# Sliding-window attention and the start of the gated delta rule: ScalarE takes the output bank, GpSimd's row products are released one by one, and the delta rule's first three steps are issued among the last attention units

## The reference, cut to what matters

```python
mod = c_act @ w_ada + b_ada                  # six vectors of 1024; the last four are made here
# attention, per block n of 128 tokens and head h
s = (q @ k_band.T) * 64**-0.5                # 128 x 256 (128 x 128 for n = 0)
mx = max(s.max(-1), sink); p = exp(s - mx)
out = (p @ v_band) / (p.sum(-1) + exp(sink - mx))
# delta rule, per chunk: products of rows with per-row scalars
kb = k * beta; vb = v * beta; kbG = kb * exp(G); qg = q * exp(G); kdec = k * exp(Glast - G)
m = strict_lower(kb @ k.T * decay); T = inverse(I + m)
v_new = T @ vb - (T @ kbG) @ S; o = qg @ S + (q @ k.T * decay) @ v_new; S = S * exp(Glast) + kdec.T @ v_new
```

## Time and profile before

| | |
|---|---|
| median of 3 runs | 2441.24 us (2441.24 to 2442.61) |
| the profiled execution's own time | 2443.43 us |
| its span | 2441.6 us |
| TensorE busy | 2299.5 us, 94% |
| VectorE, ScalarE, GpSimd busy | 877.3, 681.6 and 671.2 us |
| mean granted TensorE clock | 0.963 |

### The profile page before, as it was taken

The page is one execution under the profiler, slowest core; times in us unless marked ns, Lnnn a source line. Parts: engine busy times, 40 slices in busy tenths (PEclk is TensorE's granted clock), DMA queues, the critical chain, the costliest instruction groups (busy, mean ns, idle before and its releaser), DMA issues.

```text
span 2441.6 us, 31297 instructions
## 1 busy us (share of the span) xinstructions
PE 2299.5 (94%) x12483; PEld 1910.5 (78%) x12484; DVE 877.3 (36%) x1367; ACT 681.6 (28%) x1028; POOL 671.2 (27%) x281
## 2 busy tenths in 40 slices
PE   6997889987999999989999999999999998999998
PEld 5885568876789999968887877888866876888787
DVE  5287644445411111243322033332735524332302
ACT  3253324333100000132222132333325324222212
POOL 0323023422000000024343334333513432444432
PEclk7998889997999999999999999999999998999999
DMA  9214500003168988602322232223313222232222
GB/s 302 69 53 138 173 1 1 1 3 104 61 212 290 303 289 290 216 18 87 103 86 87 104 104 88 86 70 121 105 60 112 90 100 87 86 102 87 87 88 94
DMA packets 220360, 278.01 MB, mean 114 GB/s; under 512 B 9703, under 2 KB 199107, under 8 KB 220260
## 3 DMA queue, kind: packets, MB, share of 16 engines
q1 hardware_dynamic: 211744, 267.49, 33.4%
q10 hardware_dynamic: 7140, 4.87, 0.7%
q0 software_dynamic: 1376, 4.26, 0.5%
HBM read 272.36 MB, written 4.24 MB: 113 GB/s over the span
## 4 chain that ended last, share of the span: by engine, by line
PE 85%; DVE 6%; ACT 2%; issue 1%; SPq 1%; DMA 1%; DVEq 1%; ACTq 1%; POOL 0%; POOLq 0%
PE bank L2517 52%; PE bank L2153 10%; PE bank L2161 5%; PE bank L1601 2%; PE bank L451 1%; PE bank L1909 1%; PE bank L1594 1%; PE bank L3301 1%; PE bank L3320 1%; SPq L353 1%; DMA ring<-in_ffn_w_down 1%; PE bank L2944 1%; PE bank L1552 1%; DMA ring<-in_w_in 0%; PE bank L2924 0%
## 5 line engine op out<-in xcount | busy, mean ns | idle before, releaser
L2517 PE MATMUL bank<-hT_high_split,ring_split 128*128 128x512 f32 x2496 | 799.7, 400 | 3.6 <-DVEq L2631 3.0
L2517 PEld LDWEIGHTS bank<-hT_high_split,ring_split 128*128 128x128 f32 x2496 | 472.2, 189 | 117.5 <-DVEq L2631 3.8
L2517 PE MATMUL bank<-hT_split,ring_split 128*128 128x512 f32 x1248 | 493.3, 395 | 0.0
L2501 POOL TENSOR_TENSOR ring_split<-ring,ring_split 128x2048 fp32r<-128x2048 f32 x60 | 277.3, 4623 | 429.9 <-ACT ring_split L2486 429.9
L2486 ACT ACTIVATE ring_split<-ring 128x2048 fp32r<-128x2048 f32 x108 | 206.9, 1916 | 650.4 <-DMA ring<-in_ffn_w_down 196.4
L2517 PE MATMUL bank<-ring_split,hid_high_split 128*128 128x512 f32 x848 | 272.2, 401 | 10.2 <-DVE hid_low_split L2641 6.9
L2517 PEld LDWEIGHTS bank<-hT_split,ring_split 128*128 128x128 f32 x1248 | 236.2, 189 | 57.3 <-issue 0.2
L2857 POOL TENSOR_TENSOR ring_split<-ring,ring_split 128x2048 fp32r<-128x2048 f32 x40 | 189.7, 4743 | 329.5 <-ACT ring_split L2486 329.5
L2153 PE MATMUL bank<-arena,ring 128*128 x2048 | 236.1, 277 | 5.2 <-issue 5.2
L2153 PEld LDWEIGHTS bank<-arena,ring 128*128 128x128 f32 x2048 | 233.4, 194 | 5.4 <-issue 5.4
L2517 PE MATMUL bank<-ring_split,hid_low_split 128*128 128x512 f32 x576 | 216.4, 400 | 0.8 <-issue 0.8
(11 more groups left out here) (490 smaller groups left out, 2857.9 us busy)
## 6 DMA issues: line engine op xcount, KB each, us to landing
ring<-in_w_in SPq DMA_DIRECT2D x45, 1024.0 KB, 5.2
ring<-in_w_gate SPq DMA_DIRECT2D x32, 1024.0 KB, 5.7
ring<-in_w_up SPq DMA_DIRECT2D x32, 1024.0 KB, 8.2
ring<-in_w_down SPq DMA_DIRECT2D x32, 1024.0 KB, 7.6
ring<-in_ffn_w_gate SPq DMA_DIRECT2D x22, 1024.0 KB, 5.4
ring<-in_ffn_w_up SPq DMA_DIRECT2D x22, 1024.0 KB, 5.3
ring<-in_ffn_w_down SPq DMA_DIRECT2D x22, 1024.0 KB, 4.8
ring<-in_w_ada SPq DMA_DIRECT2D x16, 1024.0 KB, 6.7
```

Of the source, the lines that this page charges most:

```text
L2501: pool.tensor_tensor(low(n), raw(n), high(n).bitcast(F32), ALU.subtract)\
L2517: mm = pe.matmul(dst, left[l], right[r], start=start and n == 0, stop=stop and n == 2)
```

## The change

- **Bank 6 is taken by ScalarE.** A new `take(n)` in `act_swa` copies bank 6 unscaled into `mixed` (once per token block, in the iteration behind the block's last unit) and signals `w_o_taken`. `outputs` on VectorE waits for that signal only, scales inside `mixed` (both operands in SBUF), and moves from j = 1 to j = 3 of the next token block, so two units later.
- **`Pw` has three buffers**, so VectorE's unit u waits for unit u-3's transposes. `ada_sum` moves to make room; some delta rule buffers move by 16 columns.
- **The row products.** The eight of kb and qg now come first, as soon as their inputs are ready. The twelve of vb, kbG and kdec are released one by one: product i waits for VectorE's half of the modulation sum of unit i (`ada_half` behind even units is new). Only `state` is cleared here.
- **The clearing of `vnew`** moves to GpSimd's step 4 of the delta rule, in front of the first L1658 and behind its waits.
- **No meeting.** TensorE issues step 0 of the delta rule behind unit 14's iteration (after waits for `g_scaled`, `g_parts` and `w_s_taken`), step 1 behind iteration 15 and in front of the last values, and the rest behind. ScalarE issues steps 0 and 1 in its iterations 14 and 15, in front of `take(3)`. VectorE issues steps 0 to 2 behind its loop and in front of the last `outputs` and of the end of the modulation vector (`dve_ada2`). GpSimd goes straight on. TensorE's step 11 waits for `w_o_taken` and `mod_ready`.

```diff
-        def meet(e):
-            e.drain().then_inc(S("meet"), 1)
-            nxt(e, "meet", 4)
...
-            if u % 2 == 1:
-                mm.then_inc(S("ada_acc"), 1)
+            mm.then_inc(S("ada_acc" if u % 2 else "ada_half"), 1)
...
-        Pw = region(23616, 1024, "p (b i k) -> p b i k", b=2, i=2)
+        Pw = [region(at, 512, "p (i k) -> p i k", i=2) for at in (23616, 24128, 27216)]
...
+                if u == len(UNITS) - 2:
+                    nxt(pe, "g_scaled")
+                    nxt(pe, "g_parts")
+                    pe.wait_ge(S("w_s_taken"), u + 1)
+                    pe_gdn(pe, 0, 1)
+            pe_gdn(pe, 1, 2)
             values(len(UNITS) - 1)
             pe_ada2_turn(pe, 15)
+            pe.wait_ge(S("w_s_taken"), len(UNITS))
...
-                if u >= 2:
+                if u >= 3:
                     nxt(dve, "w_p_turned")
...
-                if n >= 1 and j == 1:
+                if n >= 1 and j == 3:
                     outputs(dve, n - 1)
                 dve_ada2_part(dve, u)
+            dve_gdn(dve, 0, 3)
             outputs(dve, NT - 1)
             dve_ada2(dve)
...
         def outputs(dve, n):
             c = slice(8 * n, 8 * n + 8)
-            dve.wait_ge(S("w_values"), 4 * (n + 1))
+            nxt(dve, "w_o_taken")
...
-            dve.tensor_tensor(mixed[:, n, 512:1024].rearrange("p (h e) -> p h e", e=HD),
-                              bank[6][:, :].rearrange("p (h e) -> p h e", e=HD),
-                              w_es[:, c].unsqueeze(2).broadcast_to([P, H, HD]), ALU.mult)\
-               .then_inc(S("w_o_taken"), 1)
+            o = mixed[:, n, 512:1024].rearrange("p (h e) -> p h e", e=HD)
+            dve.tensor_tensor(o, o, w_es[:, c].unsqueeze(2).broadcast_to([P, H, HD]), ALU.mult)
...
+            def take(n):
+                act.wait_ge(S("w_values"), NPAIR * (n + 1))
+                act.activation(mixed[:, n, 512:1024], bank[6][:, :], ACT.Copy).then_inc(S("w_o_taken"), 1)
...
                 act_ada2(act, u)
+                if u % NPAIR == 0 and u:
+                    take(u // NPAIR - 1)
+                if u >= len(UNITS) - 2:
+                    act_gdn(act, u - len(UNITS) + 2, u - len(UNITS) + 3)
+            take(NT - 1)
...
+            nxt(pool, "g_normed")
             nxt(pool, "g_beta")
+            scaled(pool, kb, kn, g_beta)
+            nxt(pool, "g_exps")
+            scaled(pool, qg, qn, g_expG)
             nxt(pool, "qkv_taken", 3 * NT)
...
+            u = 0
+            for dst, src, by in ((vb, vb, g_beta), (kbG, kb, g_expG), (kdec, kn, g_kdec)):
+                for t in range(NT):
+                    nxt(pool, "ada_acc" if u % 2 else "ada_half")
+                    scaled(pool, dst, src, by, (t,))
+                    u += 1
             pool.memset(state, 0.0)
-            pool.memset(vnew, 0.0)
...
+                    if s == X1:
+                        pool.memset(vnew, 0.0)
                     pool.tensor_tensor(MTl[u % 3], MT[u % 2], four(con(f"level{LEVELS[n]}")), ALU.mult)\
                         .then_inc(S("g_Ml"), 1)
```

More of the change, by code:

```diff
@@ L1011, in dve_swa @@
                 nxt(dve, "w_scores")
-                if u >= 2:
+                if u >= 3:
                     nxt(dve, "w_p_turned")
                 for i in range(2):
-                    s = dve.scalar_tensor_tensor(Pw[:, u % 2, i, 0:w], bank[2 * (u % 2) + i][:, 0:w],
+                    s = dve.scalar_tensor_tensor(Pw[u % 3][:, i, 0:w], bank[2 * (u % 2) + i][:, 0:w],
                                                  w_ss[:, n, 2 * j + i:2 * j + i + 1], mask[:, 2 * P - w:2 * P], ALU.mult, ALU.add)
@@ L1098, in build @@
         MTl = [region(24128 + 512 * b, 512, unit_of, c=P) for b in range(3)]
[L1099 to L1102, removed]
+        DT = [region(25680 + 512 * b, 512, unit_of, c=P) for b in range(2)]
+        gU = region(26704, 512, unit_of, c=P)
+        vnew = region(27216, 1024, "p (c n) -> p c n", c=2)
+        state = region(28240, 512, "p (j e) -> p j e", e=P)
         LEVELS = (2, 4, 8, 16, 32)
@@ L1137, in dve_gdn_gate, with scaled @@
             dve.scalar_tensor_tensor(g_g, g_s, -1.0, g_ea, ALU.mult, ALU.mult).then_inc(S("g_ready"), 1)
-        def scaled(e, dst, src, by):
-            for t in range(NT):
+        def scaled(e, dst, src, by, tiles=range(NT)):
+            for t in tiles:
                 i = e.tensor_tensor(dst[:, t, :].rearrange("p (h e) -> p h e", e=HD),
@@ L1304, in pe_w_gdn @@
             if g == 0:
+                if t == 0:
+                    nxt(pe, "w_o_taken")
+                    nxt(pe, "mod_ready")
                 if t:
@@ L1539, in dve_end_step, with pe_gdn @@
                 dve_gdn_turned(dve, 3, 6)
-        def pe_gdn(pe):
-            for s in range(N_STEP):
+        def pe_gdn(pe, first, last):
+            for s in range(first, last):
                 b = b_step(s)
@@ L1604, in pe_gdn, with act_gdn @@
                 pe_end_step(pe, s)
-        def act_gdn(act):
-            for s in range(N_STEP):
+        def act_gdn(act, first, last):
+            for s in range(first, last):
                 b = b_step(s)
@@ L1670, in pool_gdn, with dve_gdn @@
                     pool_wo(pool, i, q)
-        def dve_gdn(dve):
-            for s in range(N_STEP):
+        def dve_gdn(dve, first, last):
+            for s in range(first, last):
                 b = b_step(s)
@@ L3500, in _ @@
             act_swa(act)
-            meet(act)
-            act_gdn(act)
+            act_gdn(act, 2, N_STEP)
             act_router_weights(act)
@@ L3538, in _ @@
             pe_swa(pe)
[L3539 to L3542 removed]
+            pe_gdn(pe, 2, N_STEP)
             pe_w_out(pe)
@@ L3578, in _ @@
             dve_swa(dve)
-            meet(dve)
-            dve_gdn(dve)
+            dve_gdn(dve, 3, N_STEP)
             dve_norm2(dve, c1(32), c1(24))
```

18 lines of the change are left out of this document (4 added, 14 removed).

## The result

The changed kernel takes **2409.43 us** (median of 4 runs, 2406.66 to 2410.63) against 2441.24 us before; the ratio is 0.9866, with a 95% interval of 0.9853 to 0.9878. It is 31.8 us faster; the prediction was 2411.2 us, 30.0 us faster. The profiled execution has a span of 2407.1 us, 34.5 us under that of before (2441.6 us).

The account below looks back on a forecast made before the run. Bound: one chain, with VectorE's L1034 waits for TensorE's last values starving ScalarE and TensorE, and low clock. 10.4 + 16.8 + 4.9 + 1.9 - 1.0 - 3 = 30.0 us saved, giving 2411.2 us; range 2402 to 2424.

Parts of the forecast that it names:

- 10.4: First token block: L451 of unit 4 starts at about 224.5 us instead of 234.85; 10.4 us saved.
- 16.8: Loop from L451 of unit 4 to unit 14: 45.1 us instead of 61.94 without the wait of outputs; 16.8 us saved.
- 4.9: The tail, L451 of unit 14 to the delta rule's first own product: 9.8 us instead of 14.69; 4.9 us saved.
- 1.9: Delta rule's first steps, up to unit 1's differences: 8.8 us instead of 10.67; 1.9 us saved, zero at low clock.
- 1.0: Clearing of vnew on GpSimd in front of L1658: between 0 and 1.0 us lost, taken as 1.0.
- Imperfect coupling: Token blocks: TensorE and VectorE leave each other no room; about 1 us lost each, 3 us in all, ends 0 and 8.
- made long before: In the tail, GpSimd was to have gU ready long before, its last product released behind unit 11; no size given.
- The paced products: Twelve GpSimd products, one per VectorE unit, put at nothing with L1015 and L1019 as cover; 13.0 us without cover.
- The clock rival: Clock still falls once a block and in the first steps: 20 us saved, 2421 us; chance 0.12.
- the other rivals: Products collide with exposed instructions, 2418 us (0.08); another chain holds units, 2422 us (0.08); old order stays, 2431 us (0.05).
- the slower side: Low clock stays on into the delta rule; if to 500 us, 82 us lost, 2493 us; chance 0.02.

Follow-up runs that it names:

- undo_pace: The changed kernel with the twelve GpSimd products of vb, kbG and kdec not held back, so 20 run in one go; 2417.23 us.
- clear_behind: The changed kernel with vnew cleared behind the first masking of unit 0 instead of in front of it; 2408.59 us.
- undo_take: The changed kernel, but VectorE again waits for a token block's last values and takes bank 6 itself, at j = 1; 2431.11 us.
- undo_merge: The changed kernel with the meeting back and the delta rule's first three steps behind it, as before; 2417.29 us.
- only_take: The kernel before with one part alone: ScalarE takes bank 6 and the outputs stand at j = 3; 2420.91 us.
- two_pw: The changed kernel with two Pw buffers, VectorE's unit u waiting for unit u-2's transposes; 2412.38 us.
- combo: The changed kernel with nine idle matmuls in the delta rule's first steps, vnew cleared behind the first masking, last outputs and dve_ada2 in step 5; 2411.26 us.

## Why the prediction was right

**The bound and the sum.** The parts add to 36.6 us up to unit 1's differences; forecast without losses were 34.0. Each of these terms held: 10.4 came as 11.3, 16.8 as 17.6, 4.9 as 5.2, 1.9 as 2.5. VectorE's unit of 4.1 to 4.3 us and TensorE's pair of 8.92 us, both read in the kernel before, are the pace after: 8.5, 9.1, 8.9, 9.6 and 8.3 us between L445s.

That the total came within 2 us is in part luck. Up to unit 1's differences the change won more than the forecast, 36.6 us against 31.0 with the 3 us for coupling. Behind that point the clock took 6.1 us (4.3 and 1.8) where the forecast had 1.0, and the routing gave 1.9 back. The prediction also said that what is saved early arrives at the end unchanged; these stretches show that it does not quite. Between the two profiles 34.5 us were saved and 30.0 forecast; the medians differ by 31.8.

**Imperfect coupling**, 3 us lost, did not come: the loop took 44.38 us, under the 45.1 without it, because VectorE was seldom late. The one wait inside it came from gU, which the prediction had only as "made long before". That it runs when the last product is done, into unit 12, was overlooked; it cost 0.6 us here, and more in the profiles in which the clock fell behind it.

**The paced products** at nothing: right within 1 us (44.38 against 43.40 us without them). Undoing them cost 7.8 us, so the collision of rows 5 is real and the pacing is what removes it. The Trainium skill ("SBUF — State Buffer", Who interferes with whom) says that a VectorE instruction with two SBUF inputs and a GpSimd instruction that reads SBUF hold each other up by an exclusive lock. The rows agree: L1021 and L483 take 602 and 881 ns in the mean in undo_pace, and 161 and 484 ns where the single product has ended by then, and L1015, whose main operand comes from a bank, is unmoved beside the products (342 ns). The number of SBUF inputs is not the whole condition in these rows, though: L1023 has one, and it goes from 0.17 to 0.96 us beside gU and to 0.93 us in undo_pace. The same section says that an instruction with two SBUF inputs does not contend with one of GpSimd that only writes SBUF; here the clearing at 287.02 us runs beside L1726 (287.61 us, 0.69 us, its usual length), which agrees.

**The clock rival** had 0.12, and part of it came true. In the loop of this profile the clock stayed at 1.00, as forecast (in clear_behind's, with the same loop, it fell once). In the first steps it fell at about 281 us, behind the gap of 1.46 us. The argument against the rival, that the change removes the gaps behind which the clock falls, left this gap out; the kernel before has it too (in front of 317.02 us), but there the clock was low already. The term "1.9 us saved, zero at low clock" was counted only up to unit 1's differences; there 2.5 us were saved, and the low clock took its price behind that point, 4.3 us up to the second L1740, of which the clearing explains at most 1.0. That stretch had no term in the sum but the clearing's. It was an error of the step that ended the comparison at 322 us, just in front of the place (about 324 us) where the kernel before went back to full clock; the changed one did not. So "saved" in the rows of the tail and of the first steps is half true: the low stretch was moved, not removed.

**What was said against the other rivals** held: with ScalarE's `take` in front of the exponentials TensorE did not wait, and the slower side did not come: the low stretch lasted some 17 us and ended by itself.

**The parts overlap.** Undone one at a time they cost 21.7, 7.8, 7.9 and 3.0 us, 40.4 in all, against 31.8 for the whole. Part of each is, as I read it, the clock, which is lower in one place or another whichever part is missing (the rows of undo_take, undo_pace and undo_merge show it); no run separates it for each part. The bank copy is shown from both sides, 20.0 us alone and 21.7 us undone. The early start is not: undo_merge's 7.9 us hold a clock of 0.61 where only_take had 1.00 with the meeting in it.

## What to carry to other kernels

An in-order engine that waits for a bank's last writer in front of its next unit's work stalls everybody; let an engine with slack copy the bank, and put the rest of the work where its inputs are long there. Here that was 20 us of 2441 by one edit. Read the pace of a stretch without the wait from the trace of before: it is the pace that comes. Count a moved gap's clock up to where both kernels are at full clock again, not up to the last changed instruction. And before putting a difference of a few us down to an edit, look whether the clock fell at the same places in both profiles, and whether a run with identical instructions there shows the other case too.

## What the runs showed of the hardware

- The clock can fall behind small gaps, and the gap's length does not tell whether it does. It fell behind 0.91 us (two_pw) and 0.64 us (clear_behind) in an otherwise full loop, and not behind 0.62 us at the same place in the changed kernel. It fell behind 1.46 us in the changed kernel and not behind the same 1.46 us in only_take, and behind 2.47 us near 504 us but not before the change.
- How long it stays low varies as much: about 3 us in only_take, 7 us in clear_behind, 17 us before and in the changed kernel. In clear_behind TensorE had no gap from 283.7 us until the clock rose at about 291; in the changed kernel it waited four times (0.57 to 0.85 us) between 284 and 296 us and was 83% busy (14.35 of 17.39 us).
- Idle matmuls in the gaps held the clock at 2.4 GHz in four profiles and in combo only until 296 us, and those that lasted longer than the gap gave back much of what they won.
- The routing takes 53.1 or 55.5 us by the clock that it meets. A difference of 2 us between two kernels of this program is not theirs by the total alone; landmarks in the profile tell it.
